# The first gate's modulation product moved from VectorE to TensorE, in four column groups

## What is computed

```
c_act = jax.nn.silu(c)
mod = (c_act @ w_mod[l] + b_mod[l])[:, None, :]
sh1, sc1, g1, sh2, sc2, g2 = jnp.split(mod, 6, axis=-1)
h = rms_norm(x, norm1_g[l]) * (1.0 + sc1) + sh1
(fq, fk, fv, ff, nq, kc, ..., ca, cg) = split_in(h @ w_in[l])
o_fox = fox_attention(...)      # 12 forget heads: logits + F[t] - F[s]
o_nsa = nsa_attention(...)      # 12 heads, compressed, selected and window branches
o_conv = conformer_conv(...)
x = x + g1 * (concat(o_fox, o_nsa, o_conv) @ w_out[l])
h = rms_norm(x, norm2_g[l]) * (1.0 + sc2) + sh2
x = x + g2 * (square(relu(h @ w_mlp1[l])) @ w_mlp2[l])
return rms_norm(x, final_g)
```

## Time and profile before

| | us |
|---|---|
| span of the profiled execution | 1208.7 |
| median of the three timed runs | 1208.82 |
| PE busy | 1155.1 (96%) |
| DVE busy | 898.4 (74%) |
| ACT busy | 607.4 (50%) |
| the 13 forget-head steps, 239.30 to 304.22 | 64.9 |
| the 25 steps of the other heads, 323.40 to 440.85 | 117.5 |

### The profile page before, as it was taken

One profiled execution on the slowest core, in us unless ns is written; L12 is line 12 of the kernel. 1 busy time (PEld: TensorE's weight loads), 2 busy tenths in 40 slices (PEclk: granted clock), 3 DMA queues, 4 the chain that ended last, 5 costly groups with the idle time before them and its releaser, 6 DMA issues.

```text
span 1208.7 us, 17358 instructions
## 1 busy us (share of the span) xinstructions
PE 1155.1 (96%) x6811; PEld 1004.8 (83%) x6811; DVE 898.4 (74%) x1025; ACT 607.4 (50%) x886; POOL 10.5 (1%) x29
## 2 busy tenths in 40 slices
PE   4998999999989998999999999999999999999996
PEld 4898988988877776999788888888888888888785
DVE  5998989988889979996865666545666545667675
ACT  6655447876755546544433444433444333444452
POOL 2000000000000000000000000000000000000000
PEclk7998999989999999999999999999999999999999
DMA  9999996547847786886666665556665556655441
GB/s 375 419 420 420 421 370 249 175 163 277 282 175 276 284 325 244 341 350 249 219 240 238 249 237 191 192 179 237 245 233 183 186 196 244 237 214 188 160 174 69
DMA packets 46329, 306.11 MB, mean 253 GB/s; under 512 B 6381, under 2 KB 8249, under 8 KB 9785
## 3 DMA queue, kind: packets, MB, share of 16 engines
q1 hardware_dynamic: 44304, 302.58, 66.6%
q10 hardware_dynamic: 1896, 2.64, 0.7%
q0 software_dynamic: 64, 0.02, 0.0%
HBM read 303.10 MB, written 2.12 MB: 253 GB/s over the span
## 4 chain that ended last, share of the span: by engine, by line
PE 72%; DVE 12%; DMA 7%; ACT 5%; issue 4%; SPq 0%; ACTq 0%; DVEq 0%
PE quad L1102 14%; PE quad L1116 11%; PE quad L1117 11%; PE quad L1118 11%; PE quad L1104 8%; DMA mod_raw<-in_w_mod 4%; PE quad L1092 4%; PE quad L1094 4%; PE quad L1093 4%; DVE w_lo L1592 3%; DVE mod_raw L1599 2%; ACT w_hi L768 2%; ACT score L831 1%; DMA first_raw<-in_w_mod 1%; ACT conv_p L808 1%
## 5 line engine op out<-in xcount | busy, mean ns | idle before, releaser
L1592 DVE TENSOR_TENSOR w_lo<-raw,w_hi 128x1024 fp32r<-128x1024 f32 (+1 forms) x372 | 446.3, 1208 | 247.6 <-ACT w_hi L768 246.9
L768 ACT ACTIVATE w_hi<-raw 128x1024 fp32r<-128x1024 f32 (+1 forms) x372 | 387.6, 1046 | 428.7 <-PE quad L1118 222.7
L1102 PE MATMUL quad<-act,w_hi 128*128 128x512 f32 x768 | 266.4, 390 | 0.0
L1092 PE MATMUL quad<-act,w_hi 128*128 128x256 f32 x760 | 218.0, 287 | 9.4 <-DVE w_lo L1592 7.1
L1104 PE MATMUL quad<-act,w_lo 128*128 128x256 f32 x768 | 216.6, 282 | 0.0
L1093 PE MATMUL quad<-act,w_hi 128*128 128x256 f32 x760 | 215.6, 284 | 0.0
L1094 PE MATMUL quad<-act,w_lo 128*128 128x256 f32 x760 | 215.4, 283 | 0.0
L1116 PE MATMUL quad<-w_hi,u_hi 128*128 128x512 f32 x496 | 196.7, 397 | 0.6 <-DVE u_lo L2061 0.6
L1118 PE MATMUL quad<-w_hi,u_lo 128*128 128x512 f32 x496 | 196.2, 396 | 0.0
L1117 PE MATMUL quad<-w_lo,u_hi 128*128 128x512 f32 x496 | 196.1, 395 | 0.0
L1102 PEld LDWEIGHTS quad<-act,w_hi 128*128 128x128 f32 x768 | 144.2, 188 | 30.3
(11 more groups left out here) (307 smaller groups left out, 1175.3 us busy)
## 6 DMA issues: line engine op xcount, KB each, us to landing
raw<-in_w_main SPq DMA_DIRECT2D x184, 1024.0 KB, 4.8
mod_raw<-in_w_mod SPq DMA_DIRECT2D x72, 1024.0 KB, 6.6
first_raw<-in_w_mod SPq DMA_DIRECT2D x14, 1024.0 KB, 14.7
late_raw<-in_w_mod SPq DMA_DIRECT2D x10, 1024.0 KB, 8.3
x_a<-in_x SPq DMA_DIRECT2D x2, 1024.0 KB, 7.2
x<-in_x SPq DMA_DIRECT2D x2, 1024.0 KB, 8.6
bias_t<-bias_scratch ACTq DMA_DIRECT2D x1, 1536.0 KB, 14.8
raw<-in_w_tail SPq DMA_DIRECT2D x4, 352.0 KB, 8.3
```

Of the source, the lines that this page charges most:

```text
L768: A(dst[:, 0:2 * width], block_half(raw, j, width), ACT.Copy).then_inc(hi_done, 1)
L1092: mm(out, hi, act_hi[:, k, :], start=begin and m % 2 == 0, stop=False, skip_group_check=True)
L1102: mm(out, w_hi[j % 4][:, cols], act_both[:, k, :, :].rearrange("p h t -> p (h t)"), start=begin, stop=False, skip_group_check=True)
L1592: TTn(lo[:, 0:2 * width], block_half(raw, j, width), hi[:, 0:2 * width].bitcast(f32), ALU.subtract)\
```

## The change

The 16 pieces of g1 get another layout in DRAM: piece n now holds all 2048 inputs for 128 of the 2048 outputs, as 16 blocks of 128x128. For each piece PE does 16 f32 matmuls (`gate_block`, 32 passes): the stationary operand is 32 copies of one column of silu(c), the moving one is a 128x128 block. Block k goes to the PSUM partitions 32*(k%4) to 32*(k%4)+31 of the unused last quarter of `head_bank`. DVE adds the 128x128 result to its columns of `acc[1]` (`gate_sum`). The bias of g1 is now put in 32 rows and the later sum over partitions is scaled by 1/32.

Which piece is a gate piece is set by `MOD_PLAN`: two in each even step of the forget heads (12), one in the first four even steps of the others (4). They stand in `scores`, after the outputs of the pair before and ahead of the scores. The DVE turns 47 to 59 that did 7 gate rows now do 7 columns. No modulation is left on DVE between turn 60 and turn 101; from NSA step 7 on there are 9 columns, in every other turn, where 16 columns stood before from NSA step 4 on. SP issues the reload of a gate buffer ahead of the weight quarter of its turn. `transposes` of the first head of the pair also waits until the DVE sums are done.

```diff
-MODS_AT |= {FOX_AT + AHEAD + t: 1 for t in (1, 3, 5, 6, 7, 9, 11)}
-MODS_AT |= {NSA_TURN + t: 1 for t in (0, 1, 4, 7, 9, 13, 14, 15, 17, 18, 19, 20, 21, 23)}
-MODS_AT |= {NSA_TURN + t: 2 for t in (5, 11)}
+MOD_PLAN |= {FOX_AT + AHEAD + t: GATE * 2 for t in (0, 2, 4, 6, 8, 10)}
+MOD_PLAN |= {NSA_TURN + t: GATE for t in (0, 2, 4, 6)}
+MOD_PLAN |= {NSA_TURN + t: COLUMN for t in (7, 9, 11, 13, 15, 17, 19, 21, 23)}
...
+                for n in GATES_AT.get(turn, ()):
+                    if MOD_NEXT[n] is not None:
+                        early_modulation(MOD_NEXT[n], n + 2)
                 if half is not None and half % 2:
                     next_quarter(half // 2 + 4)
...
-                pool.wait_ge(mod_step, (1, MOD_G2 + 1)[s])
+                pool.wait_ge(mod_step, (3 * MOD_FIRST, MOD_G2 + 1)[s])
...
-                pool.dma_start(a[0:1, :], bmod_d[s:s + 1, :]).then_inc(acc_init[s], 16)
+                rows = (32, 1)[s]
+                pool.dma_start(a[0:rows, :], bmod_d[s:s + 1, :].to_broadcast([rows, D])).then_inc(acc_init[s], 16)
...
-                A(acc[1][:, cg * GW:(cg + 1) * GW], spare[:, :], ACT.Copy).then_inc(gate_row, 1)
+                A(acc[1][:, cg * GW:(cg + 1) * GW], spare[:, :], ACT.Copy, scale=D_CONV / 32.0).then_inc(gate_row, 1)
...
-            def scores(first):
+            def gate_block(m):
+
+                n = GATE_MODS.index(m)
+                src, full, arrivals = mod_buffer(m)
+                pe.wait_ge(full, arrivals)
+                for k in range(KT):
+                    rows = slice(32 * (k % 4), 32 * (k % 4 + 1))
+                    last = mm(head_bank[n % 2][rows, 3 * P:4 * P], c_act[:, k:k + 1].to_broadcast([P, 32]),
+                              src[:, k * P:(k + 1) * P], start=k < 4, stop=k >= KT - 4, skip_group_check=True)
+                last.then_inc(pe_block, 1)
+
+            def scores(first, gates):
...
+                for m in gates:
+                    gate_block(m)
...
-            def transposes(a):
+            def transposes(a, gates):
                 pe.wait_ge(p_ready, a + 1)
+                if gates:
+                    pe.wait_ge(mod_step, gates[-1] + 2)
...
+            def gate_sum(m):
+
+                n = GATE_MODS.index(m)
+                if n == 0:
+                    dve.wait_ge(acc_init[0], 16)
+                dve.wait_ge(pe_block, n + 1)
+                cols = slice(n * P, (n + 1) * P)
+                TTn(acc[1][:, cols], acc[1][:, cols], head_bank[n % 2][:, 3 * P:4 * P], ALU.add).then_inc(mod_step, 1)
...
                     if scored is not None:
                         bias_scores(scored)
                         bias_scores(scored + 1)
+                        for n in GATES_AT.get(turn, ()):
+                            gate_sum(n)
```

More of the change, by code:

```diff
@@ L166 @@
 MOD_FIRST = 8
-MOD_G1 = 2 * KT
-MOD_H2 = 3 * KT
 MOD_G2 = 5 * KT
-MODS_AT = {turn: 1 + (turn in (9, 21, 27, 33)) for turn in range(5, 60, 2) if turn != 45}
-MODS_AT |= {FOX_AT + AHEAD + t: 1 for t in (1, 3, 5, 6, 7, 9, 11)}
-MODS_AT |= {NSA_TURN + t: 1 for t in (0, 1, 4, 7, 9, 13, 14, 15, 17, 18, 19, 20, 21, 23)}
-MODS_AT |= {NSA_TURN + t: 2 for t in (5, 11)}
-MOD_LATE = 64
+COLUMN, GATE = "c", "g"
+MOD_PLAN = {turn: COLUMN * (1 + (turn in (9, 21, 27, 33))) for turn in range(5, 60, 2) if turn != 45}
+MOD_PLAN |= {FOX_AT + AHEAD + t: GATE * 2 for t in (0, 2, 4, 6, 8, 10)}
+MOD_PLAN |= {NSA_TURN + t: GATE for t in (0, 2, 4, 6)}
+MOD_PLAN |= {NSA_TURN + t: COLUMN for t in (7, 9, 11, 13, 15, 17, 19, 21, 23)}
+MOD_LATE = 64
+MODS = [(turn, kind) for turn in sorted(MOD_PLAN) for kind in MOD_PLAN[turn]]
+MODS_AT = {turn: len(MOD_PLAN[turn]) for turn in MOD_PLAN}
+GATE_MODS = [MOD_FIRST + i for i, (_, kind) in enumerate(MODS) if kind == GATE]
+GATES_AT = {turn: [MOD_FIRST + i for i, at in enumerate(MODS) if at == (turn, GATE)] for turn in MOD_PLAN}
+COLUMN_MODS = [m for m in range(MOD_G2) if m not in GATE_MODS]
+assert len(GATE_MODS) == KT
 MOD_SLOT = {m: m % 4 for m in range(8, 20)} | {m: (m - 20) % 3 for m in range(20, 28)}
@@ L390, in build @@
         pe_mod = sem("pe_mod")
+        pe_block = sem("pe_block")
         c_sig = sem("c_sig")
@@ L613, in _ @@
                 for _ in range(MODS_AT.get(turn, 0)):
-                    if MOD_NEXT[m] is not None:
+                    if m not in GATE_MODS and MOD_NEXT[m] is not None:
                         early_modulation(MOD_NEXT[m], m + 2)
@@ L1375, in gate_rows @@
             def gate_rows(cg):
-                pe.wait_ge(mod_step, MOD_H2 + 1)
-                mm(spare[:, :], ones[:, :], acc[1][:, cg * GW:(cg + 1) * GW], start=True, stop=True)\
+                pe.wait_ge(mod_step, GATE_MODS[-1] + 2)
+                mm(spare[:, :], ones_conv[:, :], acc[1][:, cg * GW:(cg + 1) * GW], start=True, stop=True)\
                     .then_inc(pe_mod, 1)
@@ L1387, in _ @@
                     if scored is not None:
-                        scores(scored)
+                        scores(scored, GATES_AT.get(slot + AHEAD, ()))
                     if transposed is not None:
-                        transposes(transposed)
-                        transposes(transposed + 1)
+                        transposes(transposed, GATES_AT.get(slot + AHEAD - 1, ()))
+                        transposes(transposed + 1, ())
                 if slot == 2:
@@ L1597, in modulation_column @@
                 dve.wait_ge(full, arrivals)
-                col = m if m < MOD_G1 else m - KT
+                col = COLUMN_MODS.index(m)
                 v.tensor_tensor_reduce(out=src[:, :], in0=src[:, :], in1=acc[0][:, :], scale=1.0, scalar=0.0,
@@ L1601, in modulation_column, with modulation_row @@
                     .then_inc(mod_step, 1)
-            def modulation_row(m, k, gate, src, full, arrivals, first=False):
+            def modulation_row(m, k, src, full, arrivals, first=False):
                 dve.wait_ge(full, arrivals)
                 if first:
-                    dve.wait_ge(acc_init[gate], 16)
+                    dve.wait_ge(acc_init[1], 16)
                 dve.wait_ge(mod_step, m + 1)
-                out = acc[1 - gate][:, :]
+                out = acc[0][:, :]
                 STT(out, src[:, :], c_act[:, bass.ds(k, 1)], out, ALU.mult, ALU.add).then_inc(mod_step, 1)
             def later_modulation(m):
-                source = mod_buffer(m)
-                if MOD_G1 <= m < MOD_H2:
-                    modulation_row(m, m - MOD_G1, 0, *source, first=m == MOD_G1)
-                else:
-                    modulation_column(m, *source)
+                if m not in GATE_MODS:
+                    modulation_column(m, *mod_buffer(m))
+            def gate_sum(m):
[5 more added lines that the diff above has]
+                TTn(acc[1][:, cols], acc[1][:, cols], head_bank[n % 2][:, 3 * P:4 * P], ALU.add).then_inc(mod_step, 1)
             def scale_shift(first, count, done, gain, at):
@@ L2134, in gate2_row @@
             def gate2_row(q, i, first=False):
-                modulation_row(q * 4 + (5 * KT + i), q * 4 + i, 1, mod_raw[i % 2], mod_full[i % 2],
+                modulation_row(q * 4 + (5 * KT + i), q * 4 + i, mod_raw[i % 2], mod_full[i % 2],
                                q * 32 + 16 * (MOD_USES[MOD_LATE - 2] + 3 + i // 2 + 1), first)
@@ L2236 @@
     w_h2, b_h2 = by_column(sh2, sc2)
+    w_g1 = mod[:, g1].reshape(KT, P, KT, P).transpose(2, 1, 0, 3).reshape(KT, P, D)
+    w_columns = np.concatenate([w_h1, w_h2])
+    w_mod_first = np.stack([w_g1[GATE_MODS.index(m)] if m in GATE_MODS else w_columns[COLUMN_MODS.index(m)]
+                            for m in range(MOD_G2)])
     names = ["fq", "fk", "fv", "f", "nq", "kc", "vc", "ks", "vs", "kw", "vw", "ng", "ca", "cg"]
@@ L2263 @@
         "c": by_partition(c, KT),
[L2264 removed]
+        "w_mod": np.concatenate([w_mod_first, mod[:, g2].reshape(KT, P, D)]),
         "b_mod_cols": np.concatenate([b_h1, b_h2], axis=1),
```

1 line of the change is left out of this document (removed).

## The result

The changed kernel takes 1214.38 us (median of 4 runs, 1213.44 to 1215.07), the kernel before 1209.31 us (median of 4, 1206.44 to 1210.13). The ratio is 1.005, with a 95% interval from 1.0036 to 1.0064: slower, by more than the 0.3% that can be told from no change. The forecast was 1220 us, its own range 1213 to 1227. The direction and the range held. Two terms of the sum did not, as the rows show: the price of a block and the waits for pieces.

A forecast was written before the change was run, and what follows sets the result against it. The prediction took both attention stages to be bound by PE, with holes that DVE makes. From 1208.7 us it took 17.5 won, added 26.6 for blocks and 2.0 for DMA: 1219.8, forecast 1220 us, range 1213 to 1227.

The forecast's parts named there:

- the price of a block: One gate block's 32 passes on PE: 1.6 us, between bounds of 0.88 and 3.5 us; 16 blocks counted.
- the waits for pieces: PE waiting for loads of gate pieces: 0.5 us in the first step, 1.5 around the fifth and sixth, together 2.0.
- forget heads, won: Time won back in the forget heads' steps: 5.9 us in the first, 0.7 in third and fourth, 4.2 in the fifth.
- other heads, won: Time won back in the other heads' stage: 5.5 us of waits and 1.2 of slow clock, 6.7 us.
- change of tile shape: Extra PE time where matmul shape changes, one per group of blocks: 10 x 0.1 = 1.0 us.
- What bounds the kernel: Both attention stages are PE stages with holes that DVE makes; PE waits 5.7 and 5.5 us for exponentials.
- First step: Forget heads: two gate blocks fill PE's 2.69 us hole, the clock holds, and all 5.9 us come back.
- the two-abreast row: Forget-gate sum at 214 us: two column groups side by side, the second starting late; by it a block takes 1.76 us.
- The rule that I weighed and set aside: Matmuls in other column groups overlap almost wholly; a block would be nearer 0.9 us and the sum 11 us lower.
- the prediction's own signs: Wrong if a block is near 0.9 or over 2 us, PE waits for pieces, or holes stay for another reason.
- The full overlap rival: Blocks at 0.88 us: 1207.8 us, or 1204.3 with everything won; chances 0.18 with part won, 0.13 with all won.
- point of decision: For full overlap to be 3.6 us faster, blocks must cost under 0.93 us each and every hole must close.

The follow-up runs named there:

- Experiment 6: Changed kernel with each gate block cut to one 128x128 matmul; waits, loads and DVE sums kept: 1208.27 us, ratio 0.999 to the kernel before.
- experiment 5: Changed kernel with the four matmuls of one column group next to each other in each block: 1227.47 us, ratio 1.0161 to the kernel before.
- experiment 10: Changed kernel with column groups 0 and 1 alternating four times in each block, then groups 2 and 3: 1219.4 us, ratio 1.01 to the kernel before.
- experiment 7: Changed kernel with the 16 matmuls of every gate block done twice: 1221.43 us, ratio 1.0107 to the kernel before.
- experiment 1: Changed kernel with the loads of gate pieces cut to 16 of 2048 columns: 1209.12 us, ratio 1.0012 to the kernel before.

## Why the prediction was right in its sign and wrong in its terms

The sum in the prediction's own order, in us of the profiled span:

| term | predicted | measured | from |
|---|---|---|---|
| forget heads, won | -10.8 | -11.0 | start of stage to start of the next, 84.1 to 90.3, less what was added |
| other heads, won | -6.7 | -7.4 | 117.45 to 114.10, less 4 blocks |
| 16 blocks | +25.6 | +14.1 | 16 x 0.88 |
| change of tile shape | +1.0 | +1.3 | 10 x 0.13 |
| waits for pieces | +2.0 | +5.9 | starts of the second blocks |
| behind the stages | 0 | +0.8 | the rest of 3.7 |
| sum | +11.1 | +3.7 | span |

- **What bounds the kernel** (right). Both stages were PE stages with holes made by DVE. The waits for exponentials fell from 5.7 to 0.3 us in the one and from 5.5 to 1.9 in the other.
- **First step** (right, but for 0.9 us). The blocks filled the hole of 2.69 us and the clock held; 0.33 us of the hole is left as idle time, at 246.35 (in the distances between starts the transposes lose 0.8). Experiment 6 shows both parts: with nothing to fill it, 1.6 us stay.
- **The price of a block: the step that failed.** "I take 1.6, near the two-abreast row, since that is what was seen." It is 0.88. The row's numbers were read rightly (one pass every 0.11 us in a group, the second stream when four of the first's eight passes were left), and the conclusion, "PE takes from no more than about four passes ahead", was drawn for all groups together. The orders of experiments 5 and 10 point to a reach of that size for each group by itself. In three orders the next group begins at the same point, with the fifth of the eight passes of the group or groups ahead: with one group ahead in the earlier trace rows (both at 214.85) and in experiment 5 (fifth pass at 354.17, next group at 354.18), and with two groups ahead in experiment 10 (239.72 and 239.73). Each such change saves 0.4 us of overlap. What is then still to start is three passes in experiment 5 and six in experiment 10. If PE took from a fixed number of passes ahead of all groups together, two abreast would overlap by half as much, and a block would take about 1.55 us (1.45 in a pair); it takes 1.35 (1.15). In the earlier trace rows the second stream was late because of its place in the program, behind eight passes of the other group; in the block, where the group changes with every matmul, no group stands behind a long run of another. That each group has a short queue of its own is the model that fits all four orders; the rows show the starts and not the queue.
- **The rule that I weighed and set aside.** That of the Trainium skill, "TensorE: Matmul & The Clock Gate", Part 3 (Packing small matmuls), with its nearly full overlap, was right here: four groups are (7.11 - 0.12) / 1.76 = 4.0 times as fast as one. The trace agrees with it once the groups alternate, and experiment 5 shows the condition.
- **The waits for pieces: mis-sized in the other direction.** 2.0 predicted, 5.9 measured. Two things were off: the round of two loads takes 7.5 to 8.8 us, not 7.1, and PE comes to the second piece 0.7 us earlier, since a block of 0.88 us and not of 1.6 stands ahead of it. With T, the end of the scores, at 254.8, the third step has the issue at T + 1.4 (1.7 predicted), the second piece usable at T + 10.2 (8.8) and PE there at T + 8.5 (9.3). So the larger part is the round itself, and it is not explained further. The other part follows from the failed step: with blocks of 2.07 us (experiment 5) and 1.76 us (experiment 7), and so longer steps, the waits are 0.2 and 0.4 us.
- **The total: in part luck.** By the prediction's own signs ("I am wrong if a block is near 0.9 us [...], if PE stands waiting for pieces") it was wrong in two places. With the block at 0.88 us and all other terms kept, its sum is 1208.3, outside its range; the waits, mis-sized the other way, bring the span up to 1212.4, and the time, which is 1.9 us over the span, to 1214.38, just inside. The reason given for "slower" was the price of the blocks. The reason measured is the waits: the blocks with their changes of shape cost less than what came back (15.4 against 18.4 us), and without the waits (experiment 1) the ratio is 1.0012. Also, the sum with the block at 1.2 to 1.9 us gives 1213 to 1225; no term stands behind the upper end of 1227. Experiment 7 is a check of the other terms: with 1.76 us a block the sum gives 1222.4, and its span is 1219.6. The span of the changed kernel came out 7.4 us below the sum: the blocks were 11.5 us cheaper, and a third of that came back as waits. The full overlap rival had the right block and gave 1207.8; it lacked 4.4 us of waits and allowed 1.5. Its point of decision, 0.93 us a block with every hole closed, was met by the block, but not by the loads, and not quite by the holes (18.4 us of the 19.5 came back).
- **Later.** Behind the stages the last 0.8 us of the span arise in one place, the stretch around the second norm, where PE goes through a time at the lower clock level. From the transposes behind DVE's `xn` to the next such transposes, before and then after (the after kernel is 2.9 us late there):

```profile
476.30:487.68 11.38, 10.88 (x79) 10.72 (x79) 11.35 (x13) 9.17 (x16) 0.00 (x0) 0.85 0.45 151
479.15:491.44 12.29, 12.20 (x78) 11.93 (x79) 12.20 (x15) 9.13 (x16) 0.00 (x0) 0.74 0.51 167
```

The stretch is 0.9 us longer, at a granted clock of 0.74 and not 0.85; the work there is the same in both kernels. From the first transposes with `rstd` to the same end it takes 10.4 to 11.8 us in the twelve traces of this case (11.1 before, 11.8 after, 10.8 in experiment 7), with the same work in all. So it reads as a difference between executions and not as a cost of the change, but no experiment was made on it.

The median grew by 5.1 us and the profiled span by 3.7. In every execution of the record that has both numbers the time is 1.8 to 2.0 us over the span (the profiled one of the changed kernel: 1214.28 and 1212.4). So the profiled execution of the kernel before, with its span of 1208.7, was one of about 1210.6 us, as slow as its slowest, and not one of the median; "the span agrees with the median of the timed runs to 0.1 us" compared two unlike things. The forecast lost nothing by it, since its terms are differences. But the terms above explain the 3.7 us between two executions; a typical execution before is 1 to 3 us shorter, and where that lies is not shown. Single executions of one kernel spread by 1 to 7 us.

## What to carry to other kernels

- When work is moved from an engine that reads a buffer late to one that reads it early, redo the buffer's round: from the last reader, through issue and landing, to the next reader. Here that round, not the arithmetic, decided between 1214 and 1207 us: 4.9 us of waits in one table, 9.2 in another and none in a third, with the same arithmetic.
- An overlap that is seen in a row holds for the order of the instructions in that row. Before scaling it, ask which instruction stood in front of the late one.
- Terms of a sum can be tied together: a cheaper block exposed waits that a dearer one had hidden. For a rival with another size in one term, all the others have to be worked out again.
- Before a span is set beside a timed median, look at one execution that has both numbers.

## What the runs showed of the hardware that was not expected

- f32 matmuls of 128x32 by 128x128 in four column groups, alternating: 0.88 us for 32 passes, against 3.5 in one group, 2.07 to 2.27 with the four matmuls of a group adjacent and 1.15 to 1.35 with two groups alternating at a time. Where a group of eight passes hands over to the next, the overlap is 0.4 us in both of these orders.
- Two loads of 1 MB issued together take 7.5 to 8.8 us until the second can be used, at a DMA share of 0.5 to 0.8. The median of all `mod_raw` loads from issue to landing is 7.3 us after.
- 16 blocks cost 5.5 us of span over one matmul in each one's place (1212.4 - 1206.9), and a second round of them 7.2 us more (1219.6 - 1212.4), though PE has 11.7 and 14.1 us more to do: waits for loads, and in the first case the lower clock level behind them, took or gave most of the rest.
- Waits of 2.2 and 2.4 us for a piece at the start of a step went with a granted clock of 0.85 and 0.84 in that step (experiment 6); in the changed kernel's steps it was 1.00.
